# The first output projection, two groups by token and turned through DRAM

## The reference

```python
y = jnp.einsum('btgc,gcd->btgd', pooled, w_grp).reshape(B, T, BRANCH_W) * scale
return (y * jax.nn.silu(g)) @ w_out            # the first output projection
...
x = x + gate * y                               # the residual, gate per channel
...
return rms_norm(x) * final_norm_g              # then the second block's rms_norm
```

## Time and profile before

| what | value |
|---|---|
| median of 3 runs | 1332.98 us (1332.78 to 1334.07) |
| the profiled execution, its own time | 1334.82 us |
| its span, first to last instruction | 1332.7 us |
| granted TensorE clock | 1.00 |
| busy: TensorE, VectorE, ScalarE, GpSimd | 99%, 72%, 55%, 15% |
| the stretch of the first output projection | 247.4 to 338.2 us |

### The profile page before, as it was taken

How to read it: one execution, slowest core, us unless ns; L and a number is a source line. 1 busy time by engine, 2 the same in 40 slices (tenths; PEclk the granted TensorE clock), 3 DMA queues, 4 the chain that set the end, 5 groups by cost and what they waited for, 6 DMA issues and landing times.

```text
span 1332.7 us, 18992 instructions
## 1 busy us (share of the span) xinstructions
PE 1326.0 (99%) x6963; PEld 1109.1 (83%) x6963; DVE 960.7 (72%) x1279; ACT 732.5 (55%) x1091; POOL 196.8 (15%) x313
## 2 busy tenths in 40 slices
PE   9999999999999999999999999999999999999999
PEld 5445999988888888888888988888888888888887
DVE  4558999988779898999676668746666566666552
ACT  2213435456766657556688775465655646565431
POOL 0000012100001000032122200002234234232000
PEclk9999999999999999999999999999999999999999
DMA  9999989885676776599866676656879889789662
GB/s 383 394 416 371 353 345 408 299 279 181 202 248 207 239 226 222 182 294 293 222 181 198 201 236 224 194 186 205 260 236 270 261 271 283 217 278 262 179 197 83
DMA packets 90354, 339.36 MB, mean 255 GB/s; under 512 B 12368, under 2 KB 12768, under 8 KB 85792
## 3 DMA queue, kind: packets, MB, share of 16 engines
q1 hardware_dynamic: 67392, 261.30, 57.7%
q0 software_dynamic: 22880, 76.94, 19.0%
HBM read 310.91 MB, written 29.38 MB: 255 GB/s over the span
## 4 chain that ended last, share of the span: by engine, by line
PE 81%; DMA 12%; DVE 5%; issue 1%; ACT 1%; SPq 0%; POOL 0%; DVEq 0%; POOLq 0%
PE acc L905 19%; PE acc L848 14%; PE acc L849 14%; PE acc L850 14%; PE acc L909 10%; DMA mod_ring<-mod_w 7%; DMA raw<-weights 5%; PE misc L1174 2%; DVE w_lo L1903 1%; PE misc L905 1%; PE misc L1164 1%; DVE mod_ring L1873 1%; PE misc L1065 1%; DVE mod_late L1873 1%; DVE gate_ring L1873 1%
## 5 line engine op out<-in xcount | busy, mean ns | idle before, releaser
L1903 DVE TENSOR_TENSOR w_lo<-raw,w_hi 128x1024 fp32r<-128x1024 f32 x392 | 471.5, 1221 | 178.7 <-ACT w_hi L1339 173.1
L1339 ACT ACTIVATE w_hi<-raw 128x1024 fp32r<-128x1024 f32 x392 | 405.4, 1054 | 321.6 <-DMA raw<-weights 234.7
L848 PE MATMUL acc<-w_hi,b_op 128*128 128x512 f32 x704 | 277.1, 394 | 0.0
L849 PE MATMUL acc<-w_lo,b_op 128*128 128x512 f32 x704 | 274.3, 390 | 0.0
L850 PE MATMUL acc<-w_hi,b_op 128*128 128x512 f32 x704 | 274.3, 390 | 0.0
L905 PE MATMUL acc<-b_op,w_hi 128*128 128x512 f32 x640 | 162.1, 395 | 0.0
L850 PEld LDWEIGHTS acc<-w_hi,b_op 128*128 128x128 f32 x704 | 132.2, 188 | 27.5
L848 PEld LDWEIGHTS acc<-w_hi,b_op 128*128 128x128 f32 x704 | 132.4, 188 | 26.3
L849 PEld LDWEIGHTS acc<-w_lo,b_op 128*128 128x128 f32 x704 | 132.4, 188 | 26.1
L905 PEld LDWEIGHTS acc<-b_op,w_hi 128*128 128x128 f32 x640 | 115.2, 189 | 21.0 <-issue 0.2
L905 PE MATMUL acc<-a_op,w_hi 128*128 128x512 f32 x448 | 113.1, 394 | 0.3 <-DVE a_op L1913 0.3
(11 more groups left out here) (314 smaller groups left out, 2012.8 us busy)
## 6 DMA issues: line engine op xcount, KB each, us to landing
raw<-weights SPq DMA_DIRECT2D x392, 512.0 KB, 5.1
mod_ring<-mod_w SPq DMA_DIRECT2D x26, 1024.0 KB, 14.4
u_ring<-weights SPq DMA_DIRECT2D x32, 512.0 KB, 14.6
gate_ring<-weights POOLq DMA_DIRECT2D x30, 512.0 KB, 8.3
mod_late<-mod_w SPq DMA_DIRECT2D x6, 1024.0 KB, 6.4
head_d<-head POOLq DMA_DIRECT2D x32, 128.0 KB, 4.3
t<-head_d POOLq DMA_DIRECT2D x32, 128.0 KB, 5.9
z_d<-z POOLq DMA_DIRECT2D x28, 128.0 KB, 4.8
```

The source lines that it names most:

```text
L848: nc.tensor.matmul(to, xh[:, t], wh, start=kt == 0, stop=False)
L849: nc.tensor.matmul(to, xh[:, t], wl, start=False, stop=False)
L1339: nc.scalar.activation(w_hi[:, m.c % HL_SLOTS], raw[:, q.c % RAW_SLOTS], ACT.Copy).then_inc(own.up(s_hi), 1)
L1903: nc.vector.tensor_tensor(w_lo[:, slot], raw[:, q.c % RAW_SLOTS], w_hi[:, slot].bitcast(F32), ALU.subtract).then_inc(own.up(s_lo), 1)
```

## The change

Groups 0 and 1 of the projection are computed by token. ScalarE copies each out of PSUM (`out_by_token`), VectorE transposes blocks of 32 x 32 (`out_turned`), GpSimd turns it through DRAM (its own `out_turned`), and VectorE adds the whole group to the residual with four instructions of 256 columns (`gated`). Groups 2 and 3 stay joined, both in `acc`. The turned tiles lie in `vo`, which is free by then, and `z_d` and `head_d[0]` are the ways through DRAM. The hand-written order of the conversions is moved to suit, the last gates are awaited once ahead of slab 15's remainder, and the waits of later turns count two turns more. The host lays out the weights of groups 0 and 1 like those of other groups by token.

```diff
-TURNS = tuple([("va", v) for v in range(4)] + [("za", 0), ("za", 1), ("za", 2)] +
+TURNS = tuple([("y", j) for j in range(2)] + [("va", v) for v in range(4)] + [("za", 0), ("za", 1), ("za", 2)] +
...
+        y_part = [vo[:, k:k + 4].rearrange("p k t -> p (k t)") for k in (8, 4)]
+        y_32 = at("y_32", [P, 4 * T], F32, vo_at + 12288)
...
# GpSimd
-            for j in (2, 3):
-                pool.wait_ge(s_gate, 29 + j)
-                x_again(j)
+            def out_turned(j):
+
+                n, through = turn_of("y", j), head_d[0] if j == 1 else z_d
+                pool.wait_ge(s_head_32, n)
+                to_dram(y_32[:], through, s_head_d)
+                if j == 0:
+                    for k in (2, 3):
+                        pool.wait_ge(s_gate, 29 + k)
+                        x_again(k)
+                pool.wait_ge(s_head_d, 64 * n)
+                from_dram(through, y_part[j], s_z_t)
+
+            out_turned(0)
             pool.dma_start(head_rows[:], rows_d.to_broadcast([P, 2 * P])).then_inc(s_rows, 16)
             pool.wait_ge(s_opnd, O_Z)
             pool.dma_start(ab_raw[:], w_ab_d.rearrange("p k c -> p (k c)")).then_inc(s_ab, 16)
+            out_turned(1)
...
# TensorE
-                        pe.wait_ge(s_free, u - U_WOUT + 1 if g < G_WOUT + 3 else u - 1)
+                        pe.wait_ge(s_free, U_WOUT + 2 * (h + 1) if g == G_WOUT + 2 else u - 1)
...
-            for j in range(4):
-                joined(G_WOUT + j, a_op, ready=None if j else lambda kt: O_H + kt // 4 + 1,
-                       fillers={6: early_sums} if j == 3 else None, order=PLAIN if j else SPLIT)
+            for j in range(2):
+                pe.wait_ge(s_free, j + 1)
+                group(None, slab_of(Num(G_WOUT + j)), pair_of_banks(j), 0, a_hi, a_lo, products=by_token,
+                      ready=None if j else lambda kt: O_H + kt // 4 + 1)
+            for j in (2, 3):
+                joined(G_WOUT + j, a_op, fillers={6: early_sums} if j == 3 else None)
...
# ScalarE
-            hi_parts(Num(N_WOUT + 9), 6)
+            def out_by_token(j):
+
+                act.wait_ge(s_used, slab_of(Num(G_WOUT + j + 1)).c)
+                to = y_part[j].rearrange("p (m a c) -> p a m c", m=GM, a=2)
+                for half in range(2):
+                    of = acc[:, j, half * GC:(half + 1) * GC].rearrange("p (m c) -> p m c", m=GM)
+                    nc.scalar.activation(to[:, half], of, ACT.Copy).then_inc(own.up(s_zs if half else s_act), 1)
+
+            hi_parts(Num(N_WOUT + 9), 3)
+            out_by_token(0)
+            hi_parts(Num(N_WOUT + 12), 3 + SLABS - 1)
 
             for j in range(4):
+                if j == 0:
+                    out_by_token(1)
+                    hi_parts(Num(N_WOUT + AHEAD + 7), 1)
...
-                else:
-                    hi_parts(n, SLABS)
+                elif j != 1:
+                    hi_parts(n if j else n + SLABS, SLABS)
...
# VectorE
+            def out_turned(j):
+
+                n = turn_of("y", j)
+                dve.wait_ge(s_zs, n)
+                for _ in range(2):
+                    dve.sem_inc(own.also(s_free), 1)
+                if j:
+                    dve.wait_ge(s_head_d, 64 * (n - 1))
+                nc.vector.transpose(y_32[:], y_part[j]).then_inc(own.up(s_head_32), 1)
+
+            def gated(j):
+
+                dve.wait_ge(s_z_t, 64 * turn_of("y", j))
+                dve.wait_ge(s_x_again[j], 16)
+                for m in range(GM):
+                    kt = 4 * j + m
+                    nc.vector.scalar_tensor_tensor(
+                        out=xres[:, kt], in0=tiles(y_part[j])[:, m], scalar=modv[:, 2 * KT + kt:2 * KT + kt + 1],
+                        in1=xres[:, kt], op0=ALU.mult, op1=ALU.add
+                            ).then_inc(own.up(s_x1 if m == GM - 1 else s_dve), 1)
+
             lo_parts(Num(N_WOUT + 9), 3)
-            gated_half(0, 0)
+            out_turned(0)
             lo_parts(Num(N_WOUT + 12), 3)
-
+            dve.wait_ge(s_gate, GATES)
+            lo_parts(Num(N_WOUT + AHEAD), SLABS - 1)
 
             for j in range(4):
-                gated_half(j, 1)
+                if j >= 2:
+                    gated_half(j, 1)
+                else:
+                    gated(j)
+                    if j == 0:
+                        out_turned(1)
+                        lo_parts(Num(N_WOUT + AHEAD + 7), 1)
+                    dve.wait_ge(s_x1, j + 1)
...
-                if j < 3:
+                if j == 0:
+                    lo_parts(n + SLABS, 4)
+                    gated_half(2, 0)
+                    lo_parts(n + 12, 2)
+                elif j == 1:
+                    lo_parts(n + 6, 2)
+                elif j == 2:
                     lo_parts(n, 4)
-                    gated_half(j + 1, 0)
+                    gated_half(3, 0)
                     lo_parts(n + 4, 4)
```

More of the change, by code:

```diff
@@ L649, in _, with to_dram, from_dram @@
                         x_again(j)
-            for j in (2, 3):
-                pool.wait_ge(s_gate, 29 + j)
-                x_again(j)
+            def to_dram(tile, through, written):
+                for a in range(4):
+                    rows = tile[32 * a:32 * a + 32].rearrange("p (n c) -> p n c", c=P)
+                    pool.dma_start(through[:, :, a], rows).then_inc(written, 16)
+            def from_dram(through, tile, done):
+                for b in range(4):
+                    of = through.rearrange("x n a c -> x (n a) c")[:, :, 32 * b:32 * b + 32]
+                    pool.dma_start(tile[32 * b:32 * b + 32].rearrange("p (k t) -> p k t", t=32), of
+                                   ).then_inc(done, 16)
+            def out_turned(j):
[9 more added lines that the diff above has]
+            out_turned(0)
             pool.dma_start(head_rows[:], rows_d.to_broadcast([P, 2 * P])).then_inc(s_rows, 16)
@@ L704, in _ @@
                 query_parts(j)
[L706 to L717, removed]
             def first_gate_turned(j):
@@ L896, in joined @@
                     if part == 0:
-                        pe.wait_ge(s_free, u - U_WOUT + 1 if g < G_WOUT + 3 else u - 1)
-                    tiles = [(part * SLAB_J + kk, sums_of(u)[:, m * GC:(m + 1) * GC],
+                        pe.wait_ge(s_free, U_WOUT + 2 * (h + 1) if g == G_WOUT + 2 else u - 1)
+                    tiles = [(part * SLAB_J + kk, acc[:, u % 2, m * GC:(m + 1) * GC],
                               slice(kk * HALF + m * P, kk * HALF + (m + 1) * P))
@@ L1612, in first_tap_v @@
             def first_tap_v(v):
-                act.wait_ge(s_z_t, 64 * (v + 1))
+                act.wait_ge(s_z_t, 64 * turn_of("va", v))
                 act.wait_ge(*own.last())
@@ L2457, in _ @@
                         if j < 3:
-                            dve.wait_ge(s_z_t, 64 * (j + 5))
+                            dve.wait_ge(s_z_t, 64 * turn_of("za", j))
                         else:
-                            dve.wait_ge(s_zs, 8)
+                            dve.wait_ge(s_zs, turn_of("za", 2) + 1)
                         add(o, o, gate_z[j][:], ALU.mult, done=s_tmp)
@@ L2618, in _ @@
                     lo_parts(n + 3, 4)
-                    dve.wait_ge(s_z_t, 64 * (i + 8))
+                    dve.wait_ge(s_z_t, 64 * (turn_of("za", 2) + i + 1))
                     gated_values(i)
@@ L2684, in build_stream @@
         b.append(joined_slabs(m, column) if (kind, j) == ("z", 3) else slabs(m, [column]))
-    rest = np.concatenate([g, grp, joined_stage(i["pool_w_out"][0], quarters), joined_stage(a, order_a[:8]),
+    rest = np.concatenate([g, grp, slabs(i["pool_w_out"][0], quarters[:2]),
+                           *[joined_slabs(i["pool_w_out"][0], c) for c in quarters[2:]], joined_stage(a, order_a[:8]),
                            *[slabs(a, [c]) for c in order_a[8:15]], joined_slabs(a, order_a[15]),
```

7 lines of the change are left out of this document (1 added, 6 removed).

## The result

| | before | after |
|---|---|---|
| median, us | 1333.53 (1332.78 to 1335.81, 4 runs) | 1342.94 (1341.03 to 1344.85, 4 runs) |
| ratio | | 1.0068, 95% interval 1.0051 to 1.0084 |
| profiled execution, span | 1334.8, 1332.7 | 1344.9, 1343.1 |

The profiled execution is the slowest of the four, 1.9 us above the median. All of the loss lies in one stretch. From this projection's first matmul (247.55 before, 246.79 after) to the first matmul of the decays' product in the next stage (358.76 before, 369.26 after) it is 111.2 us before and 122.5 after. Behind that matmul 973.9 us of span are left before, 973.8 after. I call this distance the stretch.

The account below looks back on a forecast made before the run. TensorE, busy 90.47 of 90.77 us, was taken to bound the kernel. -1.16 - 0.54 + 2.65 = +0.95, called 1.0, put on the median 1332.98 gave 1334.0 us; range for 8 in 10: 1331.3 to 1337.0.

Parts of the forecast that it names:

- The form by token saves 1.16, the early quarter 0.54: TensorE, groups 0 and 1: fewer matmuls save 1.16 us; no third-slab wait for the operand's third quarter saves 0.54.
- No engine gets more load, ScalarE's evictions fit: This projection: VectorE swaps 6.6 us of work for 5.8; ScalarE's two evictions of 1.26 us fit into idle time.
- The 2 MB more of traffic lie in a stretch of 232 GB/s, priced below through the turns: DMA during this projection: the turns' added bytes were counted only through how long a turn takes.
- the floor of +0.55: Group 2's second half cannot begin before 319.6, however early the turned data arrive; this alone gives +0.55 us.
- the +1.0: Whole kernel: the forecast net loss, +0.95 us called 1.0, with chance 0.56.
- Paced by the four raw slots: landing 5.1 + 1.06 + 1.22 = 7.4: Lo (VectorE's slab remainder) 15 to 21: 7.4 us from one lo to the lo four slabs on; lo 21 ends at 291.3.
- Turn of 17.5 us: Group through DRAM, VectorE's transpose to data: 1.54 us to first write, 7.0 to first read, 9.0 to data.
- slow turn: Rival, chance 0.20: second turn as slow as the worst row, data at 315.2 instead of 310.4, +5.8 us, 1338.8.
- Hi 30 needs slab 22 used, so ScalarE is free at 311.8: ScalarE's rounding of slab 30, ahead of group 1's operand, waits until TensorE has used slab 22 at 310.6.
- From group 1's residual to the half 7.9 us behind its end: VectorE: 5.5 us of operand, squares and adds, then two lo's of 2.35, before group 2's second half at 320.0.
- Only the last fold is noticed: TensorE waits some 2.65 us at the last sums for VectorE's last fold of squares; earlier group ends have slack.
- a wait at slab 28: Sign of being wrong: TensorE waiting there means the turns or the order cost more; half ends 321.7, wanted 324.6.

Follow-up runs that it names:

- the early turn: The changed kernel with the second eviction, transpose and so the second turn put ahead of slabs 19 to 21: 1339.33 us, ratio 1.0036.
- long runs: The changed kernel without the wait for the turns, their transfers moving the same bytes in runs of 4 KB: 1341.49 us, ratio 1.0059.
- one_light: The changed kernel with only group 0 by token, groups 1 to 3 joined, residual reloads held until remainders 18 and 19: 1335.83 us, ratio 1.0017.

## Why the prediction was wrong, step by step

- **The form by token saves 1.16, the early quarter 0.54**: right. No wait at the third slab, group 2 begins 1.68 us earlier in the projection's own time.
- **No engine gets more load, ScalarE's evictions fit**: right, and beside the point.
- **"The 2 MB more of traffic lie in a stretch of 232 GB/s, priced below through the turns"**: this step failed. The average of 69% over 91 us hid 21 us at 0.81, five of them, from 280 us, at 0.95; and a transfer's own duration is not what it costs. It costs what the slabs beside it lose: 7.7 us, where this sentence put nothing. The sum without traffic holds: the run without transfers lies 1.3 us above the kernel before (-0.5 to +2.8). What belongs beside it is the floor of +0.55, as that run waits for no turn, and not the +1.0. TensorE waits 2.0 us at the last sums, where the floor makes it 2.25. By the stretch it is +2.4 and not +1.3; 1.6 of these lie behind the last sums, where the clock fell in that profile.
- **"Paced by the four raw slots: landing 5.1 + 1.06 + 1.22 = 7.4"**: the rule was right, the size wrong. 5.1 was the median of the whole program, and of 271 to 292 us too as long as no turn ran there. With a landing of 8.3 the cycle is 10.6 us for four slabs, which TensorE uses up in 4 x 2.72 = 10.9: hardly anything is caught up any more, and at 9, by the same estimate, it falls behind. From the end of lo 13 to that of lo 17 it took 11.5 us, to lo 21 another 10.2 (9.0 and 11.7 in the second profile). Lo 21 ended at 297.0 and not at 291.3, so the second turn began 5.6 us late (3.9 in the second profile).
- **Turn of 17.5 us**: 298.5 to 317.0, 18.5 in the first profile, 20.1 in the second. The write leg was as forecast, 6.4 and 6.9 us for 7.0; the read leg, from first read to use, took 10.5 and 11.6 us for 9.0. The data came 6.6 and 6.5 us after the forecast 310.4, 1.0 and 2.6 of it by the turn and the rest by its late start. That my "slow turn" comes nearer to the time than the other cases is luck: it put all of its lateness on the turn, and the run without the wait wins nothing by taking that away.
- **"Hi 30 needs slab 22 used, so ScalarE is free at 311.8"**: hi 30 waited for its landing, not its slot, and ended at 318.9. In the run without transfers it was as forecast. This made a second holder, which is why taking away the turn's wait wins nothing and the early turn only 4 us.
- **From group 1's residual to the half 7.9 us behind its end**: right where ScalarE's slabs were there in time: 317.0 to 326.6, 316.9 to 326.4 again, 313.0 to 322.6 with the early turn, 309.1 to 318.7 without transfers, each 9.5 to 9.6 from start to start. Where slabs 29 and 30 alone were late it is more: 12.9 in the run without the wait, 11.4 with long runs.
- **Only the last fold is noticed**: wrong at this size. The half's end at 328.2 is 4.3 us too late for slab 28, my margin there was 2.9. The prediction had named a wait at slab 28 as a sign of being wrong.

The sum by measured parts: +1.3 for everything but the traffic, +7.7 for the traffic, 9.0 of 9.4, each good to some 2 us. Of the traffic, 6.3 hang on the two reads; small runs account for about 1.7, not clear of noise. 2 to 3 us of the change's loss go away if the reloads, which the kernel before has too, leave the first turn. What stays open is how the 7.7 divide between slabs 15 to 21 and slabs 27 to 30, since a cure for the first delayed the second; whether the reads hurt by their place or by their direction; and what decides whether the clock falls behind a wait of 1.7 us.

## What to carry to other kernels

A stream of weights with few slots lives on the difference between its cycle (landing and conversion) and the rate at which TensorE eats it: work out at what landing time it stops catching up (here, by an estimate, 4 x 2.72 - 1.06 - 1.22 = 8.6 us), and ask of every new transfer what share the DMA engines already have in those very 10 us, not over the stage. When a change is late at one place, look for the second thing that is late there before curing the first. And a reduction for a later sum goes into its engine's idle time ahead of the stream's work, if its inputs are there.

## What the hardware showed that I had not expected

Landing times are long once the share is near 1: at 271 to 292 us 512 KB took 5.1 us (median) at a share of 0.81 and 259 GB/s, 8.3 us at 1.01 and 321 GB/s. One profile does not fix the figure: five profiles with the same transfers, all at 1.00 or 1.01, have 7.0, 7.3, 8.3, 8.3 and 8.9. Nor does the mean share of a stretch: it is 6.2 us at 0.79 without the turns and 5.8 at 0.93 with their writes alone. The granted clock behind a wait is not settled by the wait: after 1.3 and 1.7 us it was 0.50 over 5 us (the lower level, 1.2 GHz) in one profile, after 0.9 and 1.7 us 1.00 in the next, while after 4.3 and 4.4 us it fell both times, to 0.80 in the lower of two stretches of 5 us. In `one_light` a single wait of 1.7 us was followed by 0.66 over 5 us. And 31 matmuls that nobody reads held it at full speed (1.00) with no gain in the median that could be measured.
